# The first third of a mixer's output projection as three rounded products, with the rounding done among the matrix heads

## What is computed

```python
y_r = jax.nn.gelu(r_g) * (o_f + flip(o_b))
y_h = _head_rms(s_f + flip(s_b), hg_norm_g) * jax.nn.silu(g_o)
y_m = jax.nn.sigmoid(m_o) * _head_ln(c_f + flip(c_b), ml_norm_g)
y = jnp.concatenate([y_r, y_h, y_m], axis=-1).astype(h.dtype)
out = jnp.einsum('bte,ed->btd', y, w_out)
...
x = _layer_norm(ALPHA * x + g1 * y, ln1_g, ln1_b)
f = _moe(x * (1 + sc2) + sh2, ...)
x = _layer_norm(ALPHA * x + g2 * f, ln2_g, ln2_b)
```

## Time and profile before

| | us |
|---|---|
| median of three runs | 728.32 (728.07 to 728.33) |
| the profiled execution | 723.59 |
| its span | 721.9 |

### The profile page before, as it was taken

How to read it: one execution, slowest core, us unless ns; L and a number is a source line. 1 busy time by engine, 2 the same in 40 slices (tenths; PEclk the granted TensorE clock), 3 DMA queues, 4 the chain that set the end, 5 groups by cost and what they waited for, 6 DMA issues and landing times.

```text
span 721.9 us, 12564 instructions
## 1 busy us (share of the span) xinstructions
PE 672.7 (93%) x4906; PEld 557.4 (77%) x4906; DVE 578.5 (80%) x850; ACT 441.6 (61%) x612; POOL 57.0 (8%) x88
## 2 busy tenths in 40 slices
PE   4699999999899999999989999999999999999981
PEld 2587998899688989965878788888888888888740
DVE  2639998798995367679388899999999999999775
ACT  1637866364223356483144689888888888888731
POOL 2060000000010001014002200000000000000220
PEclk9899999999999999999999999999999999999996
DMA  9999596635786599959937999999999999999542
GB/s 321 364 247 334 184 351 234 229 126 201 269 275 199 200 393 406 334 161 331 221 122 273 336 394 400 399 400 399 400 398 400 399 400 399 399 399 399 197 162 87
DMA packets 91325, 219.17 MB, mean 304 GB/s; under 512 B 3339, under 2 KB 3635, under 8 KB 91271
## 3 DMA queue, kind: packets, MB, share of 16 engines
q1 hardware_dynamic: 84928, 199.24, 75.0%
q0 software_dynamic: 5840, 18.94, 8.1%
q10 hardware_dynamic: 503, 0.28, 0.1%
HBM read 179.08 MB, written 39.36 MB: 303 GB/s over the span
## 4 chain that ended last, share of the span: by engine, by line
PE 75%; DVE 15%; ACT 3%; DMA 3%; issue 2%; SPq 1%; DVEq 0%; ACTq 0%
PE ps L1214 71%; DMA ring<-in_w_in 3%; PE ps L1654 2%; DVE w_lo L1817 2%; DVE arena L1977 1%; DVE arena L1976 1%; PE ps L1673 1%; DVE arena L1922 1%; ACT w_hi L843 1%; SPq L562 1%; DVE arena L2165 1%; DVE arena L2391 1%; DVE arena L2160 1%; DVE arena L2393 1%; DVE ln_stats L2151 0%
## 5 line engine op out<-in xcount | busy, mean ns | idle before, releaser
L2293 DVE TENSOR_TENSOR w_lo<-ring,w_hi 128x1024 fp32r<-128x1024 f32 x96 | 114.0, 1219 | 8.3 <-ACT w_hi L1098 7.8
L2293 DVE TENSOR_TENSOR w_lo<-arena,w_hi 128x1024 fp32r<-128x1024 f32 x96 | 113.6, 1219 | 5.6 <-ACT w_hi L1098 5.3
L1098 ACT ACTIVATE w_hi<-ring 128x1024 fp32r<-128x1024 f32 x96 | 100.5, 1062 | 19.2 <-PE ps L1214 19.0
L1098 ACT ACTIVATE w_hi<-arena 128x1024 fp32r<-128x1024 f32 x96 | 101.1, 1065 | 14.9 <-PE ps L1214 14.7
L1214 PE MATMUL ps<-h_hi,w_lo 128*128 128x384 f32 x288 | 101.5, 352 | 7.9 <-DVE w_lo L1817 6.1
L1214 PE MATMUL ps<-w_hi,slot_tokens_lo 128*128 128x512 f32 x256 | 102.6, 401 | 0.8 <-DVE w_lo L2293 0.8
L1214 PE MATMUL ps<-w_hi,slot_tokens_hi 128*128 128x512 f32 x256 | 100.2, 391 | 0.0
L1214 PE MATMUL ps<-w_lo,slot_tokens_hi 128*128 128x512 f32 x256 | 99.8, 390 | 0.0
L1214 PE MATMUL ps<-h_hi,w_hi 128*128 128x384 f32 x288 | 97.3, 338 | 0.0
L1214 PE MATMUL ps<-h_lo,w_hi 128*128 128x384 f32 x288 | 97.2, 337 | 0.0
L1817 DVE TENSOR_TENSOR w_lo<-ring,w_hi 128x1024 fp32r<-128x1024 f32 x44 | 53.6, 1225 | 23.3 <-ACT w_hi L843 22.3
(11 more groups left out here) (393 smaller groups left out, 1162.2 us busy)
## 6 DMA issues: line engine op xcount, KB each, us to landing
slot_rows<-arena SPq DMA_DIRECT2D x12, 2048.0 KB, 18.4
ring<-in_w_in SPq DMA_DIRECT2D x11, 2048.0 KB, 10.2
ring<-in_w_ada SPq DMA_DIRECT2D x10, 2048.0 KB, 9.1
ring<-in_w_gate SPq DMA_DIRECT2D x8, 2048.0 KB, 18.2
ring<-in_w_up SPq DMA_DIRECT2D x8, 2048.0 KB, 18.4
arena<-in_w_up SPq DMA_DIRECT2D x8, 2048.0 KB, 18.5
ring<-in_w_down SPq DMA_DIRECT2D x8, 2048.0 KB, 14.6
arena<-in_w_gate SPq DMA_DIRECT2D x8, 2048.0 KB, 18.3
```

The lines of the kernel that those rows point to most:

```text
L1098: act.activation(w_hi[:, at_ % 4, :], raw[:, q * QUARTER:(q + 1) * QUARTER], ACT.Copy).then_inc(S["hi_ready"], 1)
L2293: tt(w_lo[:, at_ % 4, :], raw[:, q * QUARTER:(q + 1) * QUARTER], w_hi[:, at_ % 4, :].bitcast(F32), ALU.subtract).then_inc(S["lo_dve"], 1)
```

## The change

The first third is also made in three rounded parts. `project` goes; `project_parts(0, ...)` takes its place. TensorE makes quarters 0 to 2 of a bank, then quarter 3 of the bank before. Quarters 0 to 2 need eight raises of `yr_done`, quarter 3 needs the ninth.

The rounding is put into the list of jobs. ScalarE's copies (`wout_hi`) are: YR in job n = 0, the weights' quarter 0 in n = 1, quarter 1 in n = 3, quarter 2 in n = 5, quarter 3 in n = 7. VectorE's subtractions (`wout_lo`) are: YR in n = 1, quarter 0 in n = 3, quarters 1 and 2 in n = 5, quarter 3 in n = 7, between `ml_out` and `ml_fin` of the last head. The low part of YR takes the place of YR, the low parts of the weights take the place of the raw ones, and the high parts lie in memory free at the time: that of YR in the place of the later sample rows, that of quarter 3 in that of the router's tiles.

So POOL loads the sample rows only after the first third is done (`wout_used` 1), and the rest of its queue stands behind that wait. VectorE waits for the same before it fills `mask`. The subtractions of the last two quarters of the last third (`out_part_lo` 6 and 7) are moved from behind the wait for `g_in` to before the wait for the position rows.

```diff
@@ -67,6 +67,9 @@
 WIN_COL = {"rx": 0, "rg": 1, "gq": 2, "gff": 3, "gfb": 4, "gi": 5, "go": 6, "mq": 7, "mk": 8, "mv": 9, "mo": 10}
 EARLY_ADA = (1, 3)
 WOUT = [21, 22, 23]
+WOUT_HI = {0: ("y",), 1: (0,), 3: (1,), 5: (2,)}
+WOUT_LO = {1: ("y",), 3: (0,), 5: (1, 2)}
+FIRST_PARTS = C + 1
 FIRST_EXPERT = 24
 TOP_BANK = 11
 TOP_SCORES = 15
@@ -145,13 +148,15 @@
         if n < 7:
             steps += [("ml_scores", n + 1), ("ml_w", n + 1)]
         if n == 7:
-            steps += [("bulk", "mo"), ("ml_out", n), ("ml_fin", n)]
+            steps += [("wout_hi", 3), ("bulk", "mo"), ("ml_out", n), ("wout_lo", 3), ("ml_fin", n)]
+        steps += [("wout_hi", x) for x in WOUT_HI.get(n, ())]
         if h and odd:
             steps += [("ml_T", h - 1), ("ml_gate", h - 1)]
         if h and not odd:
             steps.append(("ml_rstd", h - 1))
         if n < 7:
             steps.append(fill[n])
+        steps += [("wout_lo", x) for x in WOUT_LO.get(n, ())]
         if n == 1:
             steps.append(("modT",))
         if h and not odd:
@@ -497,12 +502,19 @@
                     for j, x in enumerate(("hi", "lo"))]
         out_lo = place("w_out_lo", o_conv + 2 * PIECE, NSLOT * PIECE, F32R).rearrange("p (s n) -> p s n", s=NSLOT)
         out_hi = place("w_out_hi", o_hg, 2 * QUARTER, F32R).rearrange("p (q n) -> p q n", q=2)
-        y_parts = [[place("yh_hi", 8 * U, U, F32R), place("yh_lo", 14 * U, U, F32R)],
+        first_hi = [place("w_out_first0", o_conv + (2 + NSLOT) * PIECE, QUARTER, F32R), None,
+                    place("w_out_first2", 6 * U, QUARTER, F32R), place("w_out_first3", o_hg + 2048, QUARTER, F32R)]
+        apart = place("w_out_first1", 7 * U + 1024, 2 * (5 * U - 512), F32R).rearrange("p (b n) -> p b n", b=2)
+        first_hi[1] = apart[:, :, 0:G]
+        y_parts = [[place("yr_hi", U, U, F32R), place("yr_lo", 13 * U, U, F32R)],
+                   [place("yh_hi", 8 * U, U, F32R), place("yh_lo", 14 * U, U, F32R)],
                    [place("ym_hi", 9 * U, U, F32R), place("ym_lo", 10 * U, U, F32R)]]
 
         def out_unit(part, k):
 
             lo = out_lo[:, WOUT[part] % NSLOT, k * QUARTER:(k + 1) * QUARTER]
+            if part == 0:
+                return first_hi[k], lo if k != 1 else lo.rearrange("p (b n) -> p b n", b=2)
             return (out_hi[:, k - 2, :] if part == 2 and k >= 2 else w_hi[:, k, :]), lo
         PICK = place("picked_rows", o_conv + 2 * PIECE, 6 * D).rearrange("p (c i d) -> p c i d", c=2, i=NT)
 
@@ -739,6 +751,7 @@
             modulation([sh2_b[0]], 1)
             pool.wait_ge(S["yh_full"], 1)
             pool.dma_start(X1[:, 0, :], a["x_prompt"][0]).then_inc(S["x2_in"], 16)
+            pool.wait_ge(S["wout_used"], 1)
             pool.dma_start(X1[:, 1:3, :], a["x_sample"][0].rearrange("(i p) d -> p i d", p=P)).then_inc(S["x2_in"], 16)
             pool.wait_ge(S["ym_done"], 2)
             pool.dma_start(pos2, a["pos"].rearrange("(i p) d -> p i d", p=P)).then_inc(S["x2_in"], 16)
@@ -1035,6 +1048,19 @@
                     act.activation(n_fin[:, 4 * d + h:4 * d + h + 1], ps[:, 2, P:P + 1], ACT.Identity).then_inc(S["cfin_sb"], 1)
                 elif kind == "ml_rstd":
                     head_rstd(job[1])
+                elif kind == "wout_hi":
+                    x = job[1]
+                    if x == "y":
+                        act.wait_ge(S["yr_done"], C)
+                        act.wait_ge(S["o_T"], NT)
+                        act.activation(y_parts[0][0], YR, ACT.Copy).then_inc(S["y_hi"], 1)
+                    else:
+                        if x == 0:
+                            act.wait_ge(ring_full[WOUT[0] % NSLOT], 16 * (WOUT[0] // NSLOT + 1))
+                        if x == 2:
+                            act.wait_ge(S["out_S"], 16)
+                        raw = ring[:, WOUT[0] % NSLOT, x * QUARTER:(x + 1) * QUARTER]
+                        act.activation(first_hi[x], raw if x != 1 else raw.rearrange("p (b n) -> p b n", b=2), ACT.Copy).then_inc(S["y_hi"], 1)
 
             def row_std(i):
 
@@ -1064,11 +1090,11 @@
             for u in range(4):
                 out_part_hi(u)
             act.wait_ge(S["yh_full"], 1)
-            act.activation(y_parts[0][0], YH, ACT.Copy).then_inc(S["y_hi"], 1)
+            act.activation(y_parts[1][0], YH, ACT.Copy).then_inc(S["y_hi"], 1)
             for u in (4, 5):
                 out_part_hi(u)
             act.wait_ge(S["ym_done"], 2)
-            act.activation(y_parts[1][0], YM, ACT.Copy).then_inc(S["y_hi"], 1)
+            act.activation(y_parts[2][0], YM, ACT.Copy).then_inc(S["y_hi"], 1)
             for u in (6, 7):
                 act.wait_ge(S["unit_used"], MIX_USED + u - 5)
                 out_part_hi(u)
@@ -1296,19 +1322,12 @@
                     last = pe.transpose(out[:, i * P:(i + 1) * P], HN[:, i, :], ident)
                 last.then_inc(S["hn_T"], 1)
 
-            def project(i, half):
-
-                for k in range(C):
-                    last = mm(ps[:, 2 * i + half, :], chunk(YR, k)[:, i * P:(i + 1) * P],
-                              slot(WOUT[0], C)[:, k, half * 512:(half + 1) * 512], k == 0, False)
-                return last
-
             def project_parts(part, k, i, half):
 
-                y = [chunk(x, k)[:, i * P:(i + 1) * P] for x in y_parts[part - 1]]
-                w = [x[:, half * 512:(half + 1) * 512] for x in out_unit(part, k)]
+                y = [chunk(x, k)[:, i * P:(i + 1) * P] for x in y_parts[part]]
+                w = [x[:, half, :] if (part, k) == (0, 1) else x[:, half * 512:(half + 1) * 512] for x in out_unit(part, k)]
                 out = ps[:, 2 * i + half, :]
-                mm(out, y[1], w[0], False, False)
+                mm(out, y[1], w[0], (part, k) == (0, 0), False)
                 hi_last = mm(out, y[0], w[0], False, False)
                 return hi_last, mm(out, y[0], w[1], False, (part, k) == (2, C - 1))
 
@@ -1548,19 +1567,23 @@
                     last.then_inc(S["z_ready"], 1)
 
             pe.wait_ge(S["z_taken"], ACT_COUNT)
-            pe.wait_ge(S["yr_done"], C)
-            full(WOUT[0])
-            for i in range(NT):
-                for half in range(2):
-                    if (i, half) == (0, 1):
-                        pe.wait_ge(S["t_taken"], H - 1)
-                    if (i, half) == (1, 0):
-                        pe.wait_ge(S["cfin_sb"], 16)
-                    if (i, half) == (1, 1):
-                        normed_T(H - 1, ps[:, 7, :])
-                    if (i, half) == (2, 1):
-                        pe.wait_ge(S["h_done"], 7)
-                    last = project(i, half)
+            pe.wait_ge(S["yr_done"], C + FIRST_PARTS - 1)
+            banks = [(i, half) for i in range(NT) for half in range(2)]
+            for n, (i, half) in enumerate(banks):
+                if (i, half) == (0, 1):
+                    pe.wait_ge(S["t_taken"], H - 1)
+                if (i, half) == (1, 0):
+                    pe.wait_ge(S["cfin_sb"], 16)
+                if (i, half) == (1, 1):
+                    normed_T(H - 1, ps[:, 7, :])
+                if (i, half) == (2, 1):
+                    pe.wait_ge(S["h_done"], 7)
+                for k in range(C - 1):
+                    project_parts(0, k, i, half)
+                if n:
+                    pe.wait_ge(S["yr_done"], C + FIRST_PARTS)
+                    project_parts(0, C - 1, *banks[n - 1])
+            _, last = project_parts(0, C - 1, *banks[-1])
             last.then_inc(S["wout_used"], 1)
 
             pe.wait_ge(S["yh_full"], 2)
@@ -2101,6 +2124,15 @@
                     normed(job[1])
                 elif kind == "ml_gate":
                     gained_head(job[1])
+                elif kind == "wout_lo":
+                    x = job[1]
+                    dve.wait_ge(S["y_hi"], 1 if x == "y" else x + 2)
+                    if x == "y":
+                        step(tt(y_parts[0][1], YR, y_parts[0][0].bitcast(F32), ALU.subtract), "yr_done")
+                    else:
+                        hi, lo = out_unit(0, x)
+                        raw = ring[:, WOUT[0] % NSLOT, x * QUARTER:(x + 1) * QUARTER]
+                        step(tt(lo, raw if x != 1 else raw.rearrange("p (b n) -> p b n", b=2), hi.bitcast(F32), ALU.subtract), "yr_done")
             normed(H - 1)
             transformed("go")
             step(tt(YH, YH, GO, ALU.mult), "yh_full")
@@ -2118,14 +2150,15 @@
 
             for u in range(4):
                 out_part_lo(u)
-            dve.wait_ge(S["y_hi"], 1)
-            tt(y_parts[0][1], YH, y_parts[0][0].bitcast(F32), ALU.subtract).then_inc(S["yh_full"], 1)
+            dve.wait_ge(S["y_hi"], FIRST_PARTS + 1)
+            tt(y_parts[1][1], YH, y_parts[1][0].bitcast(F32), ALU.subtract).then_inc(S["yh_full"], 1)
             for x, v in enumerate((SC2, SH2)):
                 cols = modc[:, 8 * v:8 * v + 8, :]
                 for s in range(2):
```

(9 more changed lines are left out.)

## The result

| | before | after |
|---|---|---|
| median, us | 727.86 (725.72 to 728.33, 6 runs) | 731.5 (730.21 to 732.99, 6 runs) |
| ratio | | 1.0048, 95% interval 1.0028 to 1.0068 |
| the profiled execution | 723.59 | 732.33 |
| its span | 721.9 | 728.6 |

The change makes the kernel about 3.6 us slower. The forecast was 726.9 and 1.4 faster, with a range to 729.4: wrong in sign, and outside its range.

A forecast was written before the change was run, and what follows sets the result against it. TensorE was taken to bound the output projection. Its first third, 21.64 us, would become 2.06 + 3.1 + 14.4 + 0.6 + 0.1, saving 1.4: 723.59 becomes 722.2, plus 4.73 gives 726.9, range 725.6 to 729.4.

The forecast's parts named there:

- the sum: Output projection's first third: 21.64 us replaced by products, wait, transposes and signal, saving 1.4; 723.59 becomes 722.2.
- the 4.73 us outside the sum: Difference between the profiled execution, 723.59, and the median of runs, 728.32; unexplained by the trace and carried over unchanged.
- rival 1: TensorE's clock halves for 3.4 us behind the 3.1 us gap, costing 1.7: 728.6 us; chance 0.2.
- The gap: TensorE's wait for VectorE's gained_head before the first third's second bank grows from 0.44 to 3.1 us.
- The stage's gain: Output projection's first third ends at 334.4 instead of 335.82, a gain of 1.4 us.
- The 0.6 in it: In the first third, about 0.6 us estimated for the last head's transposes and changes between fp32 and rounded products.
- The heads: Rounding copies and subtractions among the heads hide in front of existing waits: 0 to 0.5 us, taken as 0.
- Rival 4: Inserted steps among the heads overrun their cover, delaying TensorE by 0.5 to 1 us: 727.7 us; chance 0.08.
- The rows: Sample load moves to about 334.9; modulation rows land at 352.9, 0.8 us before VectorE needs them, costing nothing.
- the 354: Sign of being wrong: VectorE's bias step, which waits for the rows, starts after 354.
- Two bytes to one for POOL: During the loads after the first third, POOL's queue moves two bytes for each one of SyncE's w_gate load.
- Rival 2: Second modulation row lands after 353.7, delaying VectorE; slower than before from 355.1, 730.2 us at 357; chance 0.15.

The follow-up runs named there:

- again: The changed kernel once more, unaltered, against the kernel before: 731.85 us, ratio 1.0056.
- after_pad: The changed kernel with ten never-executed fp32 products in TensorE's skipped branch body, against the kernel before: 727.58 us, ratio 0.9994.
- after: The changed kernel as first measured and profiled, against the kernel before: median 731.5 us, ratio 1.0048.
- loads_last: The changed kernel with the sample rows' load and its wait moved behind POOL's other loads, against the kernel before: 730.81 us, ratio 1.0040.
- after_noif: The changed kernel without TensorE's conditional body (two further expert passes, skipped by this input), against the kernel before: 727.67 us, ratio 0.9990.
- before_noif: The kernel before without TensorE's conditional body (two further expert passes, skipped by this input), against the kernel before: 727.0 us, ratio 0.9969.

## Why the prediction was wrong, point by point

**The step that failed** is the one behind the sum: 723.59 less 1.4, and the 4.73 us outside the sum carried over "unchanged". I compared only what the changed stage does and took everything behind it, and the time around the span, as a constant. The change also adds instructions to TensorE's program (24 more recorded matmuls with their weight loads), and they move all code behind them. That costs 4.1 us together (`again` against `after_pad`, by the means): 1.1 around the span and 3.0 in it. In the four traces without padding the stops for issue are 1.6 to 3.7 us. A part of the first stop would be there anyway (0.8 to 1.9 us in the padded kernels); on the other hand TensorE runs at a granted clock of 0.5 behind the stops, from 697.98 to 704.81 in `again`, where the kernel with the gap filled has 697.71 to 701.12. From the last rounded product of the last expert to the start of the last mixing row `again` takes 18.20 us (694.83 to 713.03), that kernel 15.23 (694.61 to 709.84). No rival of mine lay outside the stage, so no width of the range could have held it for the right reason.

**The second step** is the weight of rival 1, below. Without the loss by the place the time would have been in the range (727.58 and 727.67), but not by the sum: the gain of 1.4 isn't in it.

**The 4.73** itself, of which I wrote that nothing in the trace says where, is for the greater part TensorE's clock. Of 101 executions of the kernel before, the fifteen with a mean granted clock of 0.982 or more, as in the profiled one, took 725.0 us on average, and the 71 below 0.979 took 728.7.

**The gap** was forecast at 3.1 with L1843's operation as its releaser, and is 3.02. Right.

**The stage's gain** was forecast at 1.4 us. It is 22.34 - 21.04 = 1.3 where the clock stays up. Right. The 0.6 in it for transposes and changes didn't follow from its rows (twelve products of 0.85 to 0.89 are 10.2 to 10.7 us of the 10.5), but it holds: in `again` the 66 steps from 320.81 to 336.50 take 15.69 us, and at 0.229 they would be 15.11.

**Rival 1, the clock,** had a chance of 0.2. In five profiled executions with the empty gap (`after`, `again`, `loads_last`, `after_pad`, `after_noif`) the granted clock fell to 0.5 right behind it in four. Below is the stretch 318 to 326 of after, of `again`, and of the kernel with the gap filled (us, busy by engine, granted clock, DMA share, GB/s):

```profile
318.00:326.00 8.00, 5.14 (x16) 4.07 (x17) 4.71 (x12) 7.24 (x9) 0.00 (x0) 0.79 0.47 137
```

```profile
318.00:326.00 8.00, 5.19 (x23) 4.24 (x24) 4.70 (x12) 7.24 (x9) 0.00 (x0) 1.00 0.44 132
```

```profile
318.00:326.00 8.00, 7.22 (x39) 6.02 (x39) 4.69 (x12) 7.26 (x8) 0.00 (x0) 1.00 0.43 134
```

With the drop the stage takes 22.59 to 22.61, without it 21.04: 1.55 us, where I had written 1.7. The price was right, the chance was not. None of the five profiled kernels with plain products has a drop in that stretch. I had held against this rival that the gap of 2.22 in the earlier trace rows showed nothing by itself; that was no evidence that full products on both sides protect. By the Trainium skill (TensorE: Matmul & The Clock Gate, "HAM oscillation"), which warns of a wait between bursts of products, the result would be this rival's. For the stage four traces of five agree, at gaps of 3.02; `again` at 3.01 does not. Over all timed runs the five kernels with the gap lose 18.6 us to the lower clock (50 runs; span times what the mean granted clock lacks of 1), the six without it and with the banks in their first order 16.9 (161 runs), a difference of 1.7, plus or minus 0.8. That grouping was made after the fact, and `after`, `again` and `loads_last` also have the stops at the mixing, in the last two with half clock for 6.8 us behind the first stop. The two with the gap and without these stops (24 runs) lose 18.3, those on their chips with neither 17.0 (106 runs): 1.3, plus or minus 1.3. So the traces say that the empty gap gives back about what the rounded products gain, and the timed runs don't contradict it. They don't prove it either: the kernel with the gap filled should lie some 1.2 us below `after_pad` and lies 0.5 below (plus or minus 1.5).

**The heads** were costed at nothing. From the end of the long TensorE piece that begins near 263.7 in the chain of waits to the first product of the projection it is 28.32 us before (285.86 to 314.18) and 28.24 after (287.27 to 315.51). Right for the weight quarters. The piece itself, the same 145 products, is longer: 22.07 us before and 23.65 after, with a granted clock of 0.5 from 264.24 to 267.66, behind an idle of 1.39 us that both kernels have. That is why the first third begins 1.3 later (315.51, and 315.46 in `again`). Five of the nine profiled kernels with the change have such a stretch near 264, none of the five with plain products. Whether the rounding of YR among the first heads brings it, or chance, no run tells. Rival 4 in its own form, steps that overrun their cover, is out.

**The rows** were forecast 18.0 us from the issue of the sample load to the last landing (334.9 to 352.9). It was 337.87 to 356.78, 18.9. Less the 1.3 by which the whole stage begins later, the bias step starts at 355.5, after the 354 that the prediction named as a sign of being wrong, and VectorE no longer waits for TensorE at the second bank: this term failed too. Two bytes to one for POOL also isn't what the earlier trace rows show, which is 0.12 MB to 0.08. With the stage as slow as it is they cost 0.05; in `again`, where the stage gained its 1.3, the bias step starts at 355.60 and the second bank is taken 0.5 later than TensorE allows. Rival 2's mechanism is there, at 0.5 us where I had given it 3.3.

**So the change's own worth** is near nothing: `after_pad` is 0.2 us below the kernel before (plus or minus 0.9), and `after_noif` 1.05 above `before_noif` (plus or minus 1.5). By the traces the gain of 1.3 goes to the clock in most executions, a little to the rows, and 0.35 to a longer time around the span (2.08 in place of 1.73), which stands in all changed kernels with padding or without the branch and for which I have no cause.

## What to carry to other kernels

An edit that adds or removes instructions on an engine with a skipped conditional body moves all code behind it. Before a change of under 1% is judged, look at that engine's last rows for "issue", at the instruction queue, and at the time around the span, and run both kernels with a few products in the skipped body. A gap of 3 us between bursts of full products on the bounding engine had a stretch of half clock behind it in four traces of five; price it so, or cover it with work that isn't waiting.

## What the hardware showed that I had not expected

Ten fp32 products of 128x128 that are never executed were worth 4.1 us of 731; twelve put into the kernel before cost it 2.9 (plus or minus 0.9), and twenty-two about nothing. Behind the skipped body the first stop for issue was up to 2.46 us, the second up to 1.97. TensorE went on 1.34 to 1.56 us after the end of the second packet of code, in all five kernels that stopped there. A fetch of 16 KB of code after the last work comes with about 1 us more around the span. That TensorE's code for the mixing crosses from one block to the next at the products where it stops is inferred from the packets' times and the counts; the addresses themselves are in no trace.
